# Experts sorted by token count on chip, whole float32 weights, and two column halves for small experts

## The chip, the cores and the metric

The kernel runs on one core of a Trainium2 chip. The metric is the device time of one execution in microseconds (us), the median of several. The core has five engines with programs of their own: TensorE (PE: matmuls, with its weight loads shown as PEld), VectorE (DVE), ScalarE (ACT), GpSimd (POOL) and SyncE (SP, which here only issues transfers), and 16 DMA engines. Engines wait for one another by semaphores.

## The reference

One decoder layer over 512 tokens of width 1024: a mixer, then a mixture of experts, each with a residual, and a last RMSNorm. The change touches the second part only:

```python
def hierarchical_moe(h, w_router_group, b_router_group, w_router_expert, b_router_expert,
                     w_expert_gate, w_expert_up, w_expert_down):
    ...
    gp, gi = lax.top_k(group_p, 1)
    ...
    ev, ei = lax.top_k(ep, TOP_K)
    ev = ev / jnp.sum(ev, axis=-1, keepdims=True)
    weights = gp * ev
    expert_id = gi * EXPERTS_PER_GROUP + ei
    combine = jnp.sum(jax.nn.one_hot(expert_id, N_EXPERTS, dtype=jnp.float32) * weights[..., None], axis=1)
    ...
    for e in range(N_EXPERTS):
        hid = jax.nn.silu(t @ w_expert_gate[e]) * (t @ w_expert_up[e])
        out = out + combine[:, e:e + 1] * (hid @ w_expert_down[e])
```

There are 32 experts in 4 groups; each token goes to 2 experts of one group, so there are 1024 pairs, 32 per expert on average. Gate and up are 1024 x 256, down is 256 x 1024, all float32: three matrices of 1.05 MB, 3.146 MB per expert, 100.7 MB in all.

## The kernel before

Everything is written engine by engine by hand; nothing is scheduled by a tool. After the mixer (some 470 us, untouched) the layer goes on as follows.

**Router.** TensorE transposes the normed tokens (`h2_tile`, L769) and makes the logits (L782). DVE picks group and experts by some 25 short operations (L2015 to L2047), TensorE counts how many earlier tokens chose the same expert (L812, L814: a token's rank in its expert), and DVE turns ranks into one-hot rows over 96 places (L2067). A product of those with the token numbers (L820) gives for each expert the up to 96 rows that it must read: `row_idx`. A token whose rank is 96 or more raises a flag (L2072 to L2095), and then a dense fallback computes all experts for all tokens at the end.

**Experts.** Experts are taken in the order 0 to 31, in a loop over groups of `UN` = 4, one buffer each (`wgu`, `wd`). All 32 have the same shape, 96 token rows, whatever their count. POOL gathers the rows from memory (L1190, `gather`; row numbers out of range are skipped) and writes the results back by a scatter (L1196, `scatter`). TensorE does per expert `e`: `ex_gu(e)` (gate and up side by side as 512 columns, 8 blocks of 128 in depth), `ex_tr(e+1)` (8 transposes of the gathered rows, L839), `ex_dn(e-1)` (down: 2 halves of 512 columns x 2 blocks), `ex_ht(e)` (2 transposes of the hidden rows, L861). Results leave PSUM through ACT (silu L1584, `ex_y` L1606) and DVE (L2108).

**Split product.** A float32 product is made from three in the type float32r: each operand is cut into a high and a low part.

```python
                pe.matmul(o, wh, xh, start=first, stop=False)
                pe.matmul(o, wh, xl, start=False, stop=False)
                return pe.matmul(o, wl, xh, start=False, stop=last)
```

These are L402 to L404 (`split_product`), used all over the kernel. The parts of the expert weights are made on chip: high by ACT (`gu_hi_half` L1562, `dn_hi_part` L1589), low by DVE (`gu_lo_half` L2007, `dn_lo_part` L2112), two halves for gate and up and one piece for down; the rows' parts likewise (L1577, L2102, L1598, L2116). DVE and ACT make expert 0's parts before they go on with the router.

**Weight transfers.** SP issues them: expert 0 after the first half of the output projection, 1 and 2 after the second, 3 after the first gather, and expert e+4's gate and up (L1002, L1003) when `ex_gu(e)` is done, its down (L1006) when `ex_dn(e)` is. SP runs in order, so a wait for a down buffer also holds the next gate.

Two program places matter besides: the transformed tokens `h2T` are stored away for the fallback (L1026) before their space is used, and the end (L2184 on) reads both results of each token back, weighs and adds them, and norms.

## Time and profile before

| | us |
|---|---|
| three runs | 834.97, 835.1, 838.05 |
| median | 835.1 |
| span of the profiled execution, first to last instruction | 836.0 |
| TensorE busy | 762.9 (91%) |
| DVE busy | 579.6 (69%) |
| ACT busy | 487.2 (58%) |
| POOL busy | 267.4 (32%) |
| transfers | 163.47 MB, mean 196 GB/s |

The profiled execution's own time is known as its span; it lies 0.9 us above the median and within the runs. Matmuls overlap in the array: each is drawn with its full length, so starts are closer together than lengths say. A busy share says nothing of which wait ends last. The granted clock of TensorE has two levels, 1.00 (2.4 GHz) and 0.50 (1.2 GHz). A plain float32 matmul appears as two records, a float32r matmul as one.

### The profile page before, as it was taken

Reading aid. Unit: us, or ns where it says so; the run is one execution under the profiler, and the core shown is the slowest. Engines: PE = TensorE matmul, PEld = TensorE weight load, DVE = VectorE, ACT = ScalarE, POOL = GpSimd, SP = SyncE. Lnnn points to the kernel's source line nnn. Section 1 sums busy time; section 2 is a strip of 40 time slices with the busy share of each in tenths; the row PEclk is TensorE's granted clock in tenths of the full one; section 3 lists DMA queues with packets and bytes.
Section 4 is the critical chain, followed back from the end, with each engine's and each line's share of the span. In section 5 each row is a group of like instructions: output and inputs, shape, how many; then the busy total and the mean of one; then the engine's idle time right before and its main releaser. Section 6 shows DMA issues by size and latency. Waiting matters only on the chain.

```text
span 836.0 us, 11559 instructions
## 1 busy us (share of the span) xinstructions
PE 762.9 (91%) x4238; PEld 604.6 (72%) x4238; DVE 579.6 (69%) x762; ACT 487.2 (58%) x680; POOL 267.4 (32%) x173
## 2 busy tenths in 40 slices
PE   4999999989999999998999549999999999999950
PEld 3788888878877988886788436777777777677730
DVE  4259879896764235645933556888888888888937
ACT  6322663842545445545313426888888888788833
POOL 2145433421512323425500031443444334442110
PEclk9999999999999999999999859999999999999995
DMA  8924320310300202094205677999999999989316
GB/s 240 321 88 153 113 72 31 110 42 13 127 13 2 102 2 102 1 350 164 47 1 201 267 269 249 360 365 372 358 375 367 375 345 349 354 346 353 111 57 257
DMA packets 50841, 163.47 MB, mean 196 GB/s; under 512 B 11321, under 2 KB 15433, under 8 KB 42351
## 3 DMA queue, kind: packets, MB, share of 16 engines
q1 hardware_dynamic: 43566, 154.47, 50.0%
q0 software_dynamic: 7232, 8.43, 3.1%
q8 instruction: 28, 0.46, 0.2%
q14 instruction: 15, 0.11, 0.0%
HBM read 154.48 MB, written 25.17 MB: 215 GB/s over the span
## 4 chain that ended last, share of the span: by engine, by line
PE 81%; DVE 6%; ACT 5%; DMA 5%; issue 2%; POOL 1%; SPq 0%; POOLq 0%; DVEq 0%; ACTq 0%
PE bank L402 22%; PE bank L404 21%; PE bank L403 21%; PE bank L839 3%; DMA wgu<-in_w_expert_up_dram 3%; PE bank L530 2%; DVE arena L2184 1%; PE bank L561 1%; PE bank L551 1%; PE bank L733 1%; PE bank L718 1%; PE bank L475 1%; DVE gu_lo L2007 1%; PE bank L584 1%; PE bank L599 1%
## 5 line engine op out<-in xcount | busy, mean ns | idle before, releaser
L2007 DVE TENSOR_TENSOR gu_lo<-wgu,gu_hi 128x2048 fp32r<-128x2048 f32 x64 | 146.4, 2288 | 25.7 <-ACT gu_hi L1562 25.4
L1103 POOL TENSOR_TENSOR w_lo<-arena,w_hi 128x1024 fp32r<-128x1024 f32 x36 | 86.1, 2396 | 211.9 <-ACT w_hi L1234 211.9
L1562 ACT ACTIVATE gu_hi<-wgu 128x2048 fp32r<-128x2048 f32 x64 | 122.1, 1910 | 27.2 <-DMA wgu<-in_w_expert_up_dram 17.2
L402 PE MATMUL bank<-h_hi,w_hi 128*128 128x512 f32 x320 | 128.2, 401 | 0.4 <-DVE arena L1796 0.4
L404 PE MATMUL bank<-h_hi,w_lo 128*128 128x512 f32 x320 | 125.0, 391 | 0.0
L403 PE MATMUL bank<-h_lo,w_hi 128*128 128x512 f32 x320 | 124.6, 389 | 0.0
L1190 POOL DMA_INDIRECT arena<-h_rows,row_idx x32 | 78.9, 2465 | 94.5 <-DVE row_idx L2078 76.8
L402 PE MATMUL bank<-gu_hi,heT_hi 128*96 128x512 f32 x256 | 103.9, 406 | 3.0 <-DVE heT_lo L2102 2.3
L404 PE MATMUL bank<-gu_hi,heT_lo 128*96 128x512 f32 x256 | 102.1, 399 | 0.0
L403 PE MATMUL bank<-gu_lo,heT_hi 128*96 128x512 f32 x256 | 101.5, 396 | 0.0
L1196 POOL DMA_INDIRECT y_rows<-arena,row_idx x32 | 42.4, 1325 | 177.7 <-ACT arena L1606 177.7
L2112 DVE TENSOR_TENSOR dn_lo<-wd,dn_hi 128x2048 fp32r<-128x2048 f32 x31 | 71.0, 2292 | 13.2 <-ACT dn_hi L1589 12.4
L1708 DVE SCALAR_TENSOR_TENSOR bank<-arena,bank 128x512 f32<-128x512 f32 x116 | 78.7, 749 | 0.1
L404 PEld LDWEIGHTS bank<-h_hi,w_lo 128*128 128x128 f32 x320 | 60.1, 188 | 13.0
L402 PEld LDWEIGHTS bank<-h_hi,w_hi 128*128 128x128 f32 x320 | 60.1, 188 | 12.9 <-DVE arena L1796 0.6
L403 PEld LDWEIGHTS bank<-h_lo,w_hi 128*128 128x128 f32 x320 | 60.2, 188 | 11.6
L1589 ACT ACTIVATE dn_hi<-wd 128x2048 fp32r<-128x2048 f32 x31 | 59.3, 1914 | 0.0
L402 PEld LDWEIGHTS bank<-gu_hi,heT_hi 128*96 128x96 f32 x256 | 41.8, 163 | 20.8 <-DVE heT_lo L2102 2.6
L1234 ACT ACTIVATE w_hi<-arena 128x1024 fp32r<-128x1024 f32 x40 | 41.4, 1052 | 23.8 <-PE bank L404 21.8
L404 PEld LDWEIGHTS bank<-gu_hi,heT_lo 128*96 128x96 f32 x256 | 41.7, 163 | 18.3
L403 PEld LDWEIGHTS bank<-gu_lo,heT_hi 128*96 128x96 f32 x256 | 42.0, 164 | 16.2
L402 PE MATMUL bank<-dn_hi,hidT_hi 128*96 128x512 f32 x124 | 50.5, 408 | 0.0
(315 smaller groups left out, 1428.8 us busy)
## 6 DMA issues: line engine op xcount, KB each, us to landing
wgu<-in_w_expert_gate_dram SPq DMA_DIRECT2D x32, 1024.0 KB, 9.3
wgu<-in_w_expert_up_dram SPq DMA_DIRECT2D x32, 1024.0 KB, 19.9
wd<-in_w_expert_down_dram SPq DMA_DIRECT2D x32, 1024.0 KB, 14.9
arena<-in_w_in_dram SPq DMA_DIRECT2D x8, 2048.0 KB, 8.5
arena<-in_x_dram SPq DMA_DIRECT2D x8, 512.0 KB, 7.8
arena<-in_w_in_dram SPq DMA_DIRECT2D x4, 1024.0 KB, 10.5
y_rows<-arena SPq DMA_DIRECT2D x8, 512.0 KB, 10.6
arena<-in_w_out_dram SPq DMA_DIRECT2D x2, 2048.0 KB, 10.3
```

The source lines that it names most:

```text
L402: pe.matmul(o, wh, xh, start=first, stop=False)
L403: pe.matmul(o, wh, xl, start=False, stop=False)
L404: return pe.matmul(o, wl, xh, start=False, stop=last)
L1103: gp.tensor_tensor(as_raw(w_lo[pslot(s)], s), raw(s), as_raw(w_hi[pslot(s)], s).bitcast(F32), ALU.subtract)\
L1190: gp.indirect_dma_start(out=hs[e % NHS][0:CAP, :], out_offset=None, in_=h2_rows, in_offset=bass.IndirectOffsetOnAxis(ap=row_idx[0:CAP, 0, ...
L1196: gp.indirect_dma_start(out=y_rows, in_=ysb[e % 2][0:CAP, :], in_offset=None, out_offset=bass.IndirectOffsetOnAxis(ap=row_idx[0:CAP, 1, e: ...
L1234: act.activation(as_raw(w_hi[pslot(s)], s), raw(s), ACT.Copy).then_inc(S["w_hi"], 1)
L1562: act.activation(gu_hi[j % 2][:, :, ks, :], wgu[j][:, :, ks, :], ACT.Copy)\
L1589: act.activation(dn_hi, wd[j], ACT.Copy).then_inc(S["w_dhi"], 1)
L1708: ins = STT(out=into, in0=upad[:, i, t:t + T], scalar=par[:, o + t:o + t + 1], in1=prev, op0=ALU.mult, op1=ALU.add)
L2007: TT(gu_lo[j][:, :, ks, :], wgu[j][:, :, ks, :], gu_hi[j % 2][:, :, ks, :].bitcast(F32), ALU.subtract)\
L2112: TT(dn_lo[j], wd[j], high.bitcast(F32), ALU.subtract).then_inc(S["w_dlo"], 1)
```

## The change

Four things change in the expert stage.

1. **Order.** Positions `s` = 0 to 31 take the place of expert numbers. Positions 0 to 3 (`NFIX`) are experts 0 to 3. For the others DVE and TensorE count tokens, rank the counts (`count`, `keys`, `rank`), and make a permutation by which the rows of all experts are sorted (`rows_e`, `sorted`). Positions 8, 14, 20 and 26 take the four largest, the others follow by falling count. SP reads the expert number of a position from `order_i` and issues the load with it. Results of position `s` are found by `row_idx` and, for narrow positions, `row_half`.
2. **Whole weights.** No weight or row is cut into parts: `ex_gu` and `ex_dn` use plain float32 matmuls, and ACT and DVE do no splitting here. ACT copies the transposed rows (`heT_copy`, `hidT_copy`); DVE only multiplies.
3. **Widths.** The eight positions in `WIDE` have 96 rows as before. The other 24 have 64 (`NARROW`): up goes to partitions 0 to 63 of the bank and gate to 64 to 127, on the two column halves of the array, 256 columns each; the two 512-column halves of down likewise. A token of rank 64 or more in a narrow position raises the flag.
4. **Buffers.** Six weight buffers (`NSLOT`) in place of four, three for gathered rows (`NHS`) in place of four. The down matrix is laid out as one piece of 8 KB per partition instead of two of 4 KB. The last norm's gain is loaded at the end.

The core of the diff:

```diff
-    UN = 4
+    NFIX = 4
+    WIDE = (0, 1, 2, 3, 8, 14, 20, 26)
+    NARROW = 64
+    NSLOT = 6
...
-        e_slot = [R_EXP + i * ESLOT for i in (2, 0, 1)] + [R_RING]
-        gu_hi = [parts(f"gu_hi{i}", R_SIG + i * KT * T, 2, KT, DE) for i in range(2)]
-        gu_lo = [parts(f"gu_lo{j}", o, 2, KT, DE) for j, o in enumerate(e_slot)]
-        wgu = [parts(f"wgu{j}", o, 2, KT, DE, dt=F32) for j, o in enumerate(e_slot)]
-        wd = [parts(f"wd{j}", o + 2 * KT * DE, JE, D, dt=F32) for j, o in enumerate(e_slot)]
-        dn_hi = parts("dn_hi", R_UP, JE, D)
-        dn_hi_end = parts("dn_hi_end", R_SIG, JE, D)
-        dn_lo = [parts(f"dn_lo{j}", o + 2 * KT * DE, JE, D) for j, o in enumerate(e_slot)]
...
+        EGU = 2 * KT * DE
+        gu_at = [R_EXP + 2 * ESLOT, R_EXP, R_EXP + ESLOT, R_RING, R_SIG, R_UP]
+        dn_at = [R_EXP + 2 * ESLOT + EGU, R_EXP + EGU, R_EXP + ESLOT + EGU, R_RING + EGU, R_SIG + EGU, R_SIG + EGU + JE * D]
...
+        wgu = [at(o, 2, KT, DE) for o in gu_at]
...
+        wd = [at(o, JE, D) for o in dn_at]
...
-        NHS = 4
-        hs = [at(o, D) for o in (R_UP + JE * D, R_UP + JE * D + D, R_S2, R_MASK)]
+        heT = [at(o2 + i * KT * CAP, KT, CAP) for i in range(2)]
+        heT_n = [at(o2 + i * KT * CAP, KT, NARROW) for i in range(2)]
+        NHS = 3
+        hs = [at(o, D) for o in (R_S2, R_S2 + D, R_MASK)]
...
+        def outs(s):
+
+            return s + 1 + sum(i <= s for i in WIDE)
+
+        def rows_of(s):
+            return CAP if s in WIDE else NARROW
...
+            b = begin("count", ("keys", 1), 5)
+            for c in range(NT):
+                pe.matmul(b[:, 0:NE], ones, Mx[:, c, :], start=(c == 0), stop=(c == NT - 1))
+            for c in range(NT):
+                ins = pe.matmul(b[0:NE, NE:NE + 1], Mx[:, c, :], ones[:, 0:1], start=(c == 0), stop=(c == NT - 1))
+            end(ins, "count", "route_mm")
+
+            b = begin("rows", ("idx_ready", 1), 4)
...
+                ins = pe.matmul(b[0:CAP, 0:2 * NFIX], row_of[:, i // NT, i % NT, :],
+                                codes[:, i // NT, i % NT, :, 0:NFIX], start=(i == 0), stop=(i == 2 * NT - 1))
...
+            b = begin("rows_e", ("perm_ready", 4), 6)
+            for q in range(2):
+                for i in range(2 * NT):
+                    ins = pe.matmul(b[0:NE, q * CAP:(q + 1) * CAP], codes[:, i // NT, i % NT, q, :],
+                                    row_of[:, i // NT, i % NT, :], start=(i == 0), stop=(i == 2 * NT - 1))
+            end(ins, "rows_e", "route_mm")
+            b = begin("sorted", ("sorted", 4), 7)
+            wait(pe, "perm_ready", 4)
+            for q in range(2):
+                pe.matmul(b[0:CAP, q * NE:(q + 1) * NE], rows_e[0:NE, q, :], perm[0:NE, :], start=True, stop=True)
+            pe.matmul(b[:, 2 * NE:3 * NE], both_e[0:NE, :, :].rearrange("p a b -> p (a b)"), perm[0:NE, :], start=True,
+                      stop=True)
+            pe.matmul(b[0:1, 3 * NE:4 * NE], e_col[0:NE, :], perm[0:NE, :], start=True, stop=True)
+            ins = pe.matmul(b[:, 4 * NE:5 * NE], ones[0:NE, :], on_diag[0:NE, :], start=True, stop=True)
+            end(ins, "sorted", "route_mm")
+            for b in range(5):
                 wait(pe, *used[b])
...
+            def ex_tr(s):
+
+                n = rows_of(s)
+                wait(pe, f"ld_h{s % NHS}", 16 * (s // NHS + 1))
+                wait(pe, "heT", s)
                 for k in range(KT):
...
+                    if n == CAP:
+                        o = bank[k // 4][:, (k % 4) * CAP:(k % 4 + 1) * CAP]
+                    else:
+                        o = bank[s % 2][:, k * NARROW:(k + 1) * NARROW]
+                    ins = pe.transpose(o, hs[s % NHS][0:n, :].rearrange("p (q k) -> p k q", k=KT)[:, k, :], ident[0:n, 0:n])
+                ins.then_inc(S["ex_tr"], 1)
...
+            def ex_gu(s):
+
+                wait(pe, "heT", s + 1)
+                wait(pe, f"ld_g{s % NSLOT}", 32 * (s // NSLOT + 1))
+                wait(pe, "ex_hid", s - 1)
+                o = bank[2 + s % 2]
                 for k in range(KT):
-                    if k % KH == 0:
-                        wait(pe, "w_glo", 2 * e + 1 + k // KH)
-                    ins = split_product(bank[2 + j % 2][0:CAP, :], (heT_hi[:, k, :], heT_lo[:, k, :]),
-                                        (gu_hi[j % 2][:, :, k, :], gu_lo[j][:, :, k, :]), k == 0, k == KT - 1)
+                    if s in WIDE:
+                        ins = pe.matmul(o[0:CAP, :], heT[s % 2][:, k, :], wgu[s % NSLOT][:, :, k, :], start=(k == 0),
+                                        stop=(k == KT - 1))
+                    else:
+                        for i, w in enumerate((wu, wg)):
+                            ins = pe.matmul(o[i * NARROW:(i + 1) * NARROW, 0:DE], heT_n[s % 2][:, k, :],
+                                            w[s % NSLOT][:, k, :], start=(k == 0), stop=(k == KT - 1))
                 ins.then_inc(S["ex_gu"], 1)
...
+            def ex_dn(s):
+
+                wait(pe, "hidT", s + 1)
+                wait(pe, f"ld_d{s % NSLOT}", 16 * (s // NSLOT + 1))
+                if s in WIDE or s - 1 in WIDE:
+                    wait(pe, "ex_y", outs(s - 1))
+                elif s > 1:
+                    wait(pe, "ex_y", outs(s - 2))
+                if s in WIDE:
+                    for hf in range(NH2):
+                        for m in range(JE):
+                            ins = pe.matmul(bank[6 + hf][0:CAP, :], hidT[:, m, :],
+                                            wd[s % NSLOT][:, m, hf * HALF:(hf + 1) * HALF], start=(m == 0),
+                                            stop=(m == JE - 1))
+                        ins.then_inc(S["ex_d"], 1)
+                else:
                     for m in range(JE):
-                        dh, dl = (w[:, m, hf * HALF:(hf + 1) * HALF] for w in (high, dn_lo[j]))
-                        ins = split_product(bank[6 + hf][0:CAP, :], (hidT_hi[:, m, :], hidT_lo[:, m, :]), (dh, dl),
-                                            m == 0, m == JE - 1)
-                    ins.then_inc(S["ex_d0" if hf == 0 else "ex_d1"], 1)
...
-            NTRIP = NE // UN
-            ex_tr(0, 0, 0)
-            trip(0, first=True)
-            with pe.Fori(1, NTRIP - 1) as g:
-                trip(g)
-            trip(NTRIP - 1, last=True)
+                        for hf in range(NH2):
+                            ins = pe.matmul(bank[6 + s % 2][hf * NARROW:(hf + 1) * NARROW, :], hidT_n[:, m, :],
+                                            wd[s % NSLOT][:, m, hf * HALF:(hf + 1) * HALF], start=(m == 0),
+                                            stop=(m == JE - 1))
+                    ins.then_inc(S["ex_d"], 1)
+
+            ex_tr(0)
+            for s in range(NE):
+                ex_gu(s)
+                if s < NE - 1:
+                    ex_tr(s + 1)
+                if s == 0:
+                    b = begin("flag", ("flag_ready", 1), 5)
+                    wait(pe, "route_dif", 3)
+                    ins = pe.matmul(b[0:1, 0:1], ones[:, 0:1], ovf[:, 0:1], start=True, stop=True)
+                    end(ins, "flag", "route_mm")
+                    wait(pe, *used[6])
+                    wait(pe, *used[7])
+                else:
+                    ex_dn(s - 1)
+                ex_ht(s)
+            ex_dn(NE - 1)
 
 
             wait(pe, "flag_ready", 1)
-            wait(pe, "ex_y", 2 * NE)
+            wait(pe, "ex_y", outs(NE - 1))
...
+            wde = a["w_expert_down"][0].rearrange("e (p m) n -> e p m n", m=JE)
...
+            expert_gu(3, 3)
+            expert_dn(3, 3)
+            wait(sp, "st_h2", 16 * NT)
+            wait(sp, "st_h2T", 16)
+            wait(sp, "sorted", 1)
+            for s in range(NFIX, NE):
+                e = sp.value_load(order_i[0:1, s:s + 1], min_val=0, max_val=NE - 1)
+                wait(sp, "ex_gu", s - NSLOT + 1)
+                expert_gu(s, e)
+                if s >= NSLOT:
+                    wait(sp, "ex_d", outs(s - NSLOT))
+                expert_dn(s, e)
+            wait(sp, "ex_gu", NE - 3)
+            sp.dma_start(gain3, a["final_norm_gain"].partition_broadcast(P)).then_inc(S["ld_part2"], 16)
...
+            def scatter(s):
+                gp.wait_ge(S["ex_y"], outs(s))
+                if s == NFIX:
+                    wait(gp, "sorted", 3)
+                if s in WIDE:
+                    gp.indirect_dma_start(out=y_rows, in_=ysb[s % 2][0:CAP, :], in_offset=None,
+                                          out_offset=bass.IndirectOffsetOnAxis(ap=row_idx[0:CAP, 1, s:s + 1], axis=0),
+                                          bounds_check=2 * T - 1, oob_is_err=False).then_inc(S[f"st_y{s % 2}"], 16)
+                else:
+                    gp.indirect_dma_start(out=y_half, in_=ysb[s % 2][:, 0:HALF], in_offset=None,
+                                          out_offset=bass.IndirectOffsetOnAxis(ap=row_half[:, s:s + 1], axis=0),
+                                          bounds_check=2 * NH2 * T - 1, oob_is_err=False).then_inc(S[f"st_y{s % 2}"], 16)
+
+            for s in range(NHS):
+                gather(s)
```

TensorE, from the end of one expert's gate and up to the next expert's, in the loop before (expert numbers e; L402 to L404 gate and up repeat eight times, of which three rows stand here):

```order
L404 MATMUL bank<-gu_hi,heT_lo 96x512
L839 MATMUL bank<-arena 128x96 x8
L402 MATMUL bank<-dn_hi,hidT_hi 96x512
L403 MATMUL bank<-dn_lo,hidT_hi 96x512
L404 MATMUL bank<-dn_hi,hidT_lo 96x512
...
L861 MATMUL bank<-arena 128x96 x2
L402 MATMUL bank<-gu_hi,heT_hi 96x512
L403 MATMUL bank<-gu_lo,heT_hi 96x512
L404 MATMUL bank<-gu_hi,heT_lo 96x512
```

and in the changed kernel around position 4, the first narrow one (L889 wide gate and up, L893 narrow, L918 wide down, L925 narrow down, L878 and L903 the transposes):

```order
L889 MATMUL bank<-arena 96x512 x8
L878 MATMUL bank<-arena 128x64 x8
L918 MATMUL bank<-arena 96x512 x4
L903 MATMUL bank<-arena 128x96 x2
L893 MATMUL bank<-arena 64x256 x16
L878 MATMUL bank<-arena 128x64 x8
L918 MATMUL bank<-arena 96x512 x4
L903 MATMUL bank<-arena 128x64 x2
L893 MATMUL bank<-arena 64x256 x16
L878 MATMUL bank<-arena 128x64 x8
L925 MATMUL bank<-arena 64x512 x4
```

The order of the four steps is kept; 24 and 12 matmuls become 8 and 4, or 16 and 4 of half the rows.

TensorE between the logits and the first expert of the changed kernel; before, only the first two lines' kinds, one product of 8 (L820) and the flag stood here:

```order
L831 MATMUL bank<-arena 128x128
L833 MATMUL bank<-arena 128x96
L833 MATMUL bank<-arena 128x64
L833 MATMUL bank<-arena 128x32
L838 MATMUL bank<-arena 128x32 x4
L840 MATMUL bank<-arena 32x1 x4
L846 MATMUL bank<-arena 96x8 x8
L852 MATMUL bank<-arena 32x96 x16
L858 MATMUL bank<-arena 96x32 x2
L859 MATMUL bank<-arena 128x32
L861 MATMUL bank<-arena 1x32
```

The counts (L838, L840), the rows by expert (L852) and the permutation (L858 to L861) are new, and stand ahead of expert 0's transposes; the flag's product moved behind expert 0's gate and up.

## Rows read from the trace of the kernel before

**Rows 1.** The page: busy times, the chain that ended last, and costly groups of instructions

```profile
PE 762.9 (91%) x4238; PEld 604.6 (72%) x4238; DVE 579.6 (69%) x762; ACT 487.2 (58%) x680; POOL 267.4 (32%) x173
...
PE bank L402 22%; PE bank L404 21%; PE bank L403 21%; PE bank L839 3%; DMA wgu<-in_w_expert_up_dram 3%; PE bank L530 2%; DVE arena L2184 1%; PE bank L561 1%; PE bank L551 1%; PE bank L733 1%; PE bank L718 1%; PE bank L475 1%; DVE gu_lo L2007 1%; PE bank L584 1%; PE bank L599 1%
...
L2007 DVE TENSOR_TENSOR gu_lo<-wgu,gu_hi 128x2048 fp32r<-128x2048 f32 x64 | 146.4, 2288 | 25.7 <-ACT gu_hi L1562 25.4
...
L402 PEld LDWEIGHTS bank<-gu_hi,heT_hi 128*96 128x96 f32 x256 | 41.8, 163 | 20.8 <-DVE heT_lo L2102 2.6
```

**Rows 2.** Busy time of each engine by stretch, then clock, DMA share, GB/s

```profile
core 0: us, PE busy (x) PEld busy (x) DVE busy (x) ACT busy (x) POOL busy (x), PEclk, DMA share, GB/s
470.00:480.00 10.00, 1.92 (x18) 1.78 (x16) 8.55 (x20) 4.17 (x4) 0.00 (x0) 0.67 1.00 408
...
490.00:500.00 10.00, 3.30 (x15) 2.40 (x15) 6.53 (x20) 4.17 (x4) 6.83 (x5) 0.50 0.42 130
...
600.00:700.00 100.00, 99.94 (x492) 73.00 (x491) 88.63 (x76) 86.67 (x98) 41.60 (x22) 1.00 0.95 363
```

**Rows 3.** The chain in order of time, experts: start us, us, what

```profile
524.88 0.86 PE bank L839 x8
...
656.29 0.86 PE bank L839 x8
```

**Rows 4.** Timeline of TensorE inside one expert: start us, us, engine, line

```profile
600.90 0.39 PE L403 MATMUL bank<-dn_lo,hidT_hi 128*96 128x512 f32 x1
601.13 0.39 PE L404 MATMUL bank<-dn_hi,hidT_lo 128*96 128x512 f32 x1
```

**Rows 5.** The chain from 224 to 240 us: plain float32 products back to back

```profile
227.46 3.72 PE bank L530 x16
231.18 3.43 PE bank L637 x8
```

**Rows 6.** Timeline of TensorE in the triangular solve: small tiles, then the full array

```profile
258.36 1.20 PE L584 MATMUL bank<-arena 32*32 32x32 f32 x64
...
259.82 0.40 PE L403 MATMUL bank<-h_lo,w_hi 128*128 128x512 f32 x1
...
266.91 2.08 PE L584 MATMUL bank<-arena 64*64 64x64 f32 x32
...
287.43 1.45 PE L584 MATMUL bank<-arena 32*32 32x32 f32 x64
```

**Rows 7.** Timeline around the router: logits, splitting, row product, first two experts

```profile
468.24 3.68 PE L782 MATMUL bank<-arena 128*128 128x64 f32 x32
...
470.91 4.49 DVE L2007 TENSOR_TENSOR gu_lo<-wgu,gu_hi 128x2048 fp32r<-128x2048 f32 x2 [3.79 <-ACT gu_hi L1562]
475.32 0.30 DVE L2016 TENSOR_TENSOR arena<-bank,arena 128x144 f32<-128x144 f32 x1
...
487.49 2.79 PE L820 MATMUL bank<-arena 128*96 128x64 f32 x16 [4.28 <-DVE arena L2067]
...
498.69 0.74 PE L402 MATMUL bank<-gu_hi,heT_hi 128*96 128x512 f32 x1 [1.17 <-DVE heT_lo L2102]
...
506.92 0.43 PE bank L839 x4
...
507.37 0.42 DVE L2108 TENSOR_TENSOR arena<-arena,bank 96x256 f32<-96x256 f32 x1 [8.74 <-ACT arena L1584]
...
512.50 0.48 PE bank L402
```

**Rows 8.** Timeline at the last expert's result

```profile
806.38 0.59 ACT L1606 ACTIVATE arena<-bank 96x512 f32<-96x512 f32 x1 [0.81 <-PE bank L404]
```

**Rows 9.** DMA queues in 600 to 650 us; up weights to landing, 528 to 540, 700 to 730

```profile
q1 hardware_dynamic: 2963, 16.82, 88.1%
q0 software_dynamic: 1228, 1.79, 9.9%
...
wgu<-in_w_expert_up_dram SPq DMA_DIRECT2D x2, 1024.0 KB, 12.0
...
wgu<-in_w_expert_up_dram SPq DMA_DIRECT2D x3, 1024.0 KB, 22.7
```

More of the change, by code:

```diff
@@ L823, in _ @@
             end(ins, "rows", "route_mm")
-            b = begin("flag", ("flag_ready", 1))
-            wait(pe, "route_dif", 3)
-            ins = pe.matmul(b[0:1, 0:1], ones[:, 0:1], ovf[:, 0:1], start=True, stop=True)
-            end(ins, "flag", "route_mm")
-            for b in range(8):
+            b = begin("rows_e", ("perm_ready", 4), 6)
[3 more added lines that the diff above has]
+                                    row_of[:, i // NT, i % NT, :], start=(i == 0), stop=(i == 2 * NT - 1))
@@ L1050, in _ @@
             wait(sp, "st_y1", 16 * NE // 2)
-            wait(sp, "ex_d1", NE)
+            wait(sp, "ex_d", outs(NE - 1))
             wait(sp, "ov_over", 1)
@@ L1207, in _ @@
+            for s in range(NHS):
+                gather(s)
+            for s in range(NE):
+                if s + NHS < NE:
+                    gather(s + NHS)
+                if s > 0:
+                    scatter(s - 1)
             scatter(NE - 1)
@@ L1630, in _, with heT_copy @@
-            act.wait_ge(S["idx_ready"], 1)
-            act.wait_ge(S["st_h2"], 16 * NT)
-            act.wait_ge(S["st_h2T"], 16)
-            gu_hi_half(1, 0, 1, 0)
-            heT_copy(0, 0, 0)
-            trip(0, first=True)
-            with act.Fori(1, NE // UN - 1) as g:
-                trip(g)
-            trip(NE // UN - 1, last=True)
+            def heT_copy(s):
+                wait(act, "ex_tr", s + 1)
+                wait(act, "ex_gu", s - 1)
+                if s in WIDE:
+                    for half in range(2):
+                        ins = act.activation(heT[s % 2][:, half * KH:(half + 1) * KH, :],
+                                             bank[half][:, 0:KH * CAP].rearrange("p (k n) -> p k n", k=KH), ACT.Copy)
+                else:
+                    ins = act.activation(heT_n[s % 2], bank[s % 2][:].rearrange("p (k n) -> p k n", k=KT), ACT.Copy)
+                ins.then_inc(S["heT"], 1)
@@ L2136, in _ @@
-            gu_lo_half(1, 0, 1, 0)
-            heT_rest(0, 0, 0)
-            trip(0, first=True)
-            with v.Fori(1, NE // UN - 1) as g:
-                trip(g)
-            trip(NE // UN - 1, last=True)
+            for s in range(NE):
+                wait(v, "ex_sil", s + 1)
+                wait(v, "ex_ht", s)
+                o = bank[2 + s % 2]
+                if s in WIDE:
+                    ins = TT(hid[0:CAP, :], sil[0:CAP, :], o[0:CAP, DE:2 * DE], ALU.mult)
+                else:
+                    ins = TT(hid[0:NARROW, :], sil[0:NARROW, :], o[0:NARROW, 0:DE], ALU.mult)
+                ins.then_inc(S["ex_hid"], 1)
```

347 lines of the change are left out of this document (149 added, 198 removed).

## The prediction

> **What bounds the kernel now.** I read the page first: TensorE is busy for 91% of the span, and the three split-product lines hold 64% of the chain that ended last [rows 1]. A mean over the span hides stages, so next the windows [rows 2]. From 600 to 700 us TensorE is busy 99.94 of 100 us at clock 1.00, and in the same 100 us the DMA share is 0.95 at 363 GB/s. From 470 to 500 both are different: the router runs, TensorE is mostly idle and its clock falls to 0.50 (the 1.2 GHz level); that is a latency stage. Third, the chain through the experts [rows 3]: the eight transposes that open each expert start at 524.88 and at 656.29 with 14 periods between, 9.386 us each. The timeline fills such a period [rows 4]: a matmul of 512 columns starts every 0.233 us though each is drawn 0.39 us long, so pace, not duration, is the price. 36 matmuls x 0.233 = 8.4, the transposes 0.86, and about 0.13 is left for the two transposes of the hidden rows. TensorE is the bound, and DMA is close behind it: the landing time of the up weights grows from 12.0 us at 528 to 540 to 22.7 us at 700 to 730 [rows 9], so transfers fall slowly behind.
>
> **The product whole.** It removes ACT's high parts and DVE's low parts of all weights (64 of 2.3 us for gate and up on DVE alone [rows 1]). Under a TensorE that never idles they cover nothing but themselves: worth 0, except at the start. On TensorE 3 split matmuls become one of plain float32. The conv mean does four of those (128x512), recorded as 8, in 3.43 us [rows 5]: 0.857 each against 3 x 0.233 = 0.70. Whole float32 alone is thus **slower**: a wide expert costs 8 x 0.857 = 6.86 and 4 x 0.857 = 3.43, 10.29 us in place of 8.4. A 256-column record costs 3.72/16 = 0.233, a 512-column one 3.43/8 = 0.43: the price goes by columns.
>
> **Column halves.** A narrow expert issues gate and up as 16 matmuls of 256 columns and down as 4 of 512, each on half of the array's columns. One after the other that is again 10.29 us; fully beside each other 5.14. The trace of before has no halves that share all rows. Nearest is the triangular solve [rows 6]: 64x64 products, one place of the array at a time, take (2.08-0.19)/31 = 0.061 us per record. 32x32 products, which alternate between two places, take (1.20-0.19)/63 = 0.016, another time (1.45-0.19)/63 = 0.020 (0.19 is one record's own length past its start). Half the columns would be 0.030 if serial, so two places give 1.5 to 1.9 times. Longer matmuls should lie near the upper end, where what is fixed per record weighs less: I take 1.8, 5.72 us per narrow expert, with 2.0 and 1.5 as ends of the range. These places share neither rows nor columns, so 1.0 is a rival. The Trainium skill ("TensorE: Matmul & The Clock Gate", Part 3, Measured speedup vs the span model) gives 2.38 times for three column tiles, 0.79 of ideal; for two that is 1.59 by my estimate, and the sum below would end at 810. No row here shows it.
>
> Going from the 32x32 places to the full array costs 259.82-0.233-259.38 = 0.2 us [rows 6]; a narrow expert has four such changes. Bounds 0 and 0.2, I take 0.1 each: 24 x 0.4 = 9.6 us.
>
> **The start.** DVE splits expert 0's weights before it turns to the logits [rows 7]: 470.91 to 475.32, while the logits are ready at 468.24+3.68 = 471.92. Gone, this gives 3.4 us, and the row product ends at 486.9 instead of 487.49+2.79 = 490.3. Then the sort is added: the transposed rows (32 records; the row product takes 2.79 for 16, less its last record's length 0.16 each: 5.2), two copies (0.6), the permutation (10 records and its hand-over: 1.9), the last two estimated from the same rows. The transposes of expert 0 stand behind them on TensorE, so they start near 494.6; the gather's flight is covered. 1.5 for them at the low clock and 1.2 for two ACT copies: gate/up of expert 0 starts at 497.3 against 498.69. It is 16 records x 0.43 = 6.9, plus 2.6 for the low clock (before: 8.2 for 24 x 0.233 = 5.6): 506.8. With transposes and expert 0's hidden rows (0.86 + 0.3), expert 1 starts at **508.0**. Before it was 512.5, since it waited for its split. The remaining router work on DVE (order, indices, codes, weights: 27 operations, none wider than the logits' 0.30 us) takes at most 9 us and ends by 504, before the first hidden rows need DVE.
>
> **The sum for TensorE from 508.0.** Wide gate/up 7 x 6.86 = 48.0; wide down 8 x 3.43 = 27.4; narrow 24 x 5.72 = 137.2; row transposes 30 x 0.86 = 25.8 (fewer columns, same weight loads); hidden transposes 31 x 0.2 = 6.2 (0.13 each before, a little more at a change of mode); changes 9.6; last hidden rows and copy, uncovered, 1.5. Together 255.7, so the last matmul ends at 763.7. Before it ended at 806.4 and the rest took 836.0-806.4 = 29.6 [rows 8], which the change leaves. Span 793.3. The span stands 0.9 above the median of the three runs (835.1), so **792 us**.
>
> Covered: silu and product are done 0.87 us after gate/up ends (506.92 to 507.79) [rows 7] and lie under the next transposes and down product (0.86 + 1.9). POOL is busy 41.6 us of 100 over 10.65 experts [rows 2], 3.9 each, which fits under 7. If that cover fails, each narrow expert grows by up to 1.
>
> **DMA under it.** In 600 to 650 us, 16.82 MB of weights is 5.35 experts, at 88.1% of 50 us: 8.2 us of all engines per expert, and 9.9% for indirect rows: 0.9 [rows 9]. From 470 to 480, with nothing indirect under way, 408 GB/s were moved [rows 2]: 3.146 MB/408 = 7.7. So 8.6 to 9.1 us per expert with rows. The sort reads its first number near 495, when expert 3's loads (issued near 492) still run, so the queue does not dry: 29 experts x 8.6 to 9.1 = 249 to 264, from 492. The wide experts at the front add gaps of about 5, since slots come free only every 11.5 us and SP waits in order (down's slot, then the next gate): last weights at 746 to 761. Six slots let DMA be five experts ahead at 550; it loses about 1 us per narrow run of the order and is not caught before the end. Thus 763.7 stands, but with little to spare.
>
> **Rivals.**
> - *Halves run one after the other.* The mechanism is shown only for places with different rows. Each narrow expert then costs 4.57 us more: 24 x 4.57 = 110, **902 us**, slower. It decides from a speed-up under 1.23 (24 x (10.29/1.23-5.72) = 43). For it: nothing here shows shared rows. Against: 1.9 times for the places shown. Chance 0.10.
> - *Weight loads are not hidden between halves.* A narrow expert has 40 records, each with a load; at 0.061 us each (the pace of the 64x64 records) 2.4 us on top of 5.14, so 24 x 1.82 = 44 more: **836 us**, no change. For it: twice as many loads per us as now. Against: in the full array loads of 163 ns vanish under a 0.233 us pace [rows 1]. Chance 0.07. The skill's rule in the same Part 3 (The mechanism) is that a load overlaps a running matmul only when its row group differs, or goes to the background buffer; the first half of it speaks against this change, and the full array's rows here show loads hidden with no row group differing.
> - *DMA becomes the bound at its present pace.* 29 x 9.4 = 273 from 492, gaps 5, last down and copy 4: 774 + 29.6 - 0.9 = **803 us**. For it: the share of 0.95 and the growing landing times. Against: 408 GB/s was reached. Chance 0.12.
> - *An expert above 64 tokens lands in a narrow position* and the dense fallback runs, over all experts and tokens: well above a millisecond. From the reference's routing, the four largest of experts 4 to 31 have 74, 66, 62 and 59 tokens, the next 57, so it can't with this input. Chance 0.01.
>
> **The numbers.** My case has 0.70. Its own ends: speed-up 2.0 and free changes of mode, 13.7 + 9.6 less, 769; speed-up 1.5 (164.6 in place of 137.2) and 0.2 per change, 37 more, 829. With DMA's 803 inside, the range 768 to 828 leaves 0.18 out. About 0.5% (4 us) is what a measurement tells here. Faster: 0.70 + 0.12 = 0.82. The 836 case is split: same 0.04, slower 0.03; with serial and fallback slower is 0.14.
>
> **What would show it.** Right: narrow gate/up takes 3.8 us for 32 records, wide 6.9; transposes every 11.5 and 7.0 us; no splitting operations; gate/up of expert 1 near 508; last matmul near 764; DMA share near 0.95 or above. Wrong: narrow gate/up of 6.9 us (serial) or 5 (loads exposed); TensorE waiting for DMA on the expert weights with its clock falling to 0.50 in the second half (DMA bound); a long wait for the order before expert 4's loads.

## The result and the profile after

| | before | after |
|---|---|---|
| median us | 836.0 (4 runs, 834.97 to 838.05) | 796.1 (4 runs, 794.36 to 798.44) |
| span of the profiled execution | 836.0 | 792.6 |
| TensorE, DVE, ACT busy | 762.9, 579.6, 487.2 | 726.7, 330.5, 292.4 |
| transfers | 163.47 MB | 163.61 MB |

Ratio 0.9535, interval [0.9515, 0.9555]: faster by 4.7%, 40 us. Forecast: 792 in 768 to 828.

The page of the changed kernel; the groups are line, engine, operation, out<-in xcount | busy, mean ns of one | idle before:

```profile
PE 726.7 (92%) x4296; PEld 528.3 (67%) x4296; DVE 330.5 (42%) x591; ACT 292.4 (37%) x536; POOL 211.7 (27%) x193
...
PE 85%; DVE 5%; ACT 4%; issue 3%; POOL 1%; DMA 1%; POOLq 0%; ACTq 0%; DVEq 0%; SPq 0%
...
L893 PE MATMUL bank<-arena 128*64 128x256 f32 x768 | 91.2, 391 | 5.2 <-issue 5.2
```

Against [rows 1], DVE lost 249 us of work and TensorE 36. All splitting of expert weights is gone, and TensorE's 36 us are most of the 43.4 us between the two spans. That fits the prediction's view that work under TensorE's cover was worth nothing by itself; no run leaves out the splitting alone. New is the 5.2 us of idle in front of L893, the narrow gate and up.

The chain through the experts, in order of time (start us, us, what), answers to [rows 3]:

```profile
505.01 6.88 PE bank L889 x16
511.88 0.86 PE bank L878 x8
512.74 3.44 PE bank L918 x8
516.18 0.20 PE bank L903 x2
516.38 6.87 PE bank L889 x16
...
594.54 3.60 PE bank L893 x32
598.14 1.02 PE bank L878 x8
599.16 1.87 PE bank L925 x8
601.03 0.38 PE bank L903 x2
601.41 3.60 PE bank L893 x32
```

A wide expert takes 516.38-505.01 = 11.37 us, a narrow one 601.41-594.54 = 6.87, against 9.39 for every expert before. Narrow gate and up, on two column halves, take 3.60 us where the wide ones take 6.88 (1.91 times), and down takes 1.87 where the wide one takes 3.44 (1.84). These ratios set 64 token rows against 96; the experiments below compare equal shapes. Eight wide and 24 narrow experts average 8.0.

Windows of the changed kernel (us, busy time of each engine, then granted clock, DMA share, GB/s), against [rows 2]:

```profile
480.00:490.00 10.00, 7.96 (x48) 7.62 (x48) 3.21 (x16) 0.00 (x0) 3.01 (x3) 0.50 0.87 318
490.00:500.00 10.00, 8.81 (x30) 4.48 (x31) 5.51 (x29) 0.87 (x2) 1.04 (x1) 0.83 0.87 325
500.00:550.00 50.00, 48.60 (x190) 23.14 (x190) 2.23 (x6) 12.78 (x27) 7.55 (x8) 1.00 1.01 379
...
600.00:650.00 50.00, 50.00 (x312) 26.79 (x310) 2.48 (x6) 12.15 (x28) 12.76 (x13) 1.00 1.02 387
650.00:700.00 50.00, 48.64 (x304) 26.65 (x301) 2.61 (x7) 11.77 (x27) 12.78 (x14) 1.00 1.02 391
700.00:740.00 40.00, 36.94 (x193) 19.39 (x193) 1.94 (x5) 8.49 (x19) 7.83 (x8) 0.91 1.00 397
```

Two things are to be read. DMA works at a share of 1.0 from 500 to about 735. And TensorE, which after one wait of 1.40 us at 503 to 504.6 (the first silu, see the last part) was not idle again until 650, then misses 1.4 of 50 and 3.1 of 40 us, with its clock at 0.91. Its timeline shows where (start us, us, engine, line, operation, and in brackets the idle time before):

```profile
687.44 3.67 PE L893 MATMUL bank<-arena 128*64 128x256 f32 x32
...
695.75 3.67 PE L893 MATMUL bank<-arena 128*64 128x256 f32 x32 [1.36 <-issue]
...
705.76 6.65 PE L893 MATMUL bank<-arena 128*64 128x256 f32 x32 [3.06 <-issue]
...
756.16 3.67 PE L893 MATMUL bank<-arena 128*64 128x256 f32 x32 [0.77 <-issue]
...
762.47 1.94 PE L925 MATMUL bank<-arena 128*64 128x512 f32 x8 [0.54 <-ACT arena L1676]
```

Three products of gate and up begin late, and the one after the 3.06 us wait takes 6.65 us in place of 3.67, at the lower clock. That is 1.36 + 3.06 + 2.98 + 0.77 = 8.2 us. The releaser is only "issue", so the trace doesn't name late weights. It does leave little else: such a product waits in the program for the copy of its transposed rows, for its gate and up weights, and for an older expert's hidden rows. Before the wait from 702.70 to 705.76 the copy was done at 701.08 and the hidden rows at 700.28. The experiments have to confirm it.

### The profile page after: what moved, and what is told of

Read it like the earlier page. It is cut to its first block, busy times and chain, and to the rows that moved or that the text cites. A ratio compares the mean times of both kernels' runs of the same rounds, so it can differ in the third digit from the quotient of the medians.

```text
span 792.6 us, 11110 instructions
## 1 busy us (share of the span) xinstructions
PE 726.7 (92%) x4296; PEld 528.3 (67%) x4296; DVE 330.5 (42%) x591; ACT 292.4 (37%) x536; POOL 211.7 (27%) x193
## 2 busy tenths in 40 slices
DMA packets 45218, 163.61 MB, mean 206 GB/s; under 512 B 9771, under 2 KB 13883, under 8 KB 32622
## 4 chain that ended last, share of the span: by engine, by line
PE 85%; DVE 5%; ACT 4%; issue 3%; POOL 1%; DMA 1%; POOLq 0%; ACTq 0%; DVEq 0%; SPq 0%
PE bank L421 13%; PE bank L423 12%; PE bank L422 12%; PE bank L893 11%; PE bank L889 7%; PE bank L925 6%; PE bank L878 4%; PE bank L918 4%; PE bank L549 2%; PE bank L903 1%; DVE arena L2239 1%; PE bank L580 1%; PE bank L570 1%; PE bank L752 1%; PE bank L737 1%
## 5 line engine op out<-in xcount | busy, mean ns | idle before, releaser
L893 PE MATMUL bank<-arena 128*64 128x256 f32 x768 | 91.2, 391 | 5.2 <-issue 5.2
L893 PEld LDWEIGHTS bank<-arena 128*64 128x64 f32 x768 | 56.2, 140 | 31.3 <-issue 7.7
L1283 POOL DMA_INDIRECT y_rows<-arena,row_half x24 | 24.3, 1011 | 133.1 <-ACT arena L1688 133.1
L889 PE MATMUL bank<-arena 128*96 128x512 f32 x128 | 58.3, 609 | 1.0 <-ACT arena L1656 1.0
L1268 POOL DMA_INDIRECT arena<-h_rows,row_idx x32 | 30.9, 966 | 91.8 <-DVE row_idx L2130 69.5
L925 PE MATMUL bank<-arena 128*64 128x512 f32 x192 | 46.5, 604 | 0.5 <-ACT arena L1676 0.5
L889 PEld LDWEIGHTS bank<-arena 128*96 128x96 f32 x128 | 20.8, 168 | 32.3 <-issue 30.9
L878 PEld LDWEIGHTS bank<-arena 64*128 64x128 f32 (+1 forms) x256 | 30.9, 201 | 14.3 <-issue 14.3
L878 PE MATMUL bank<-arena 64*128 64x64 f32 (+1 forms) x256 | 35.0, 277 | 0.0
L1217 POOL TENSOR_TENSOR b_lo<-arena,b_hi 128x512 fp32r<-128x512 f32 x16 | 25.6, 1601 | 31.0 <-ACT b_hi L1561 31.0
## 6 DMA issues: line engine op xcount, KB each, us to landing
y_rows<-arena SPq DMA_DIRECT2D x8, 512.0 KB, 10.3
```

The source lines that it names most:

```text
L878: ins = pe.transpose(o, hs[s % NHS][0:n, :].rearrange("p (q k) -> p k q", k=KT)[:, k, :], ident[0:n, 0:n])
L889: ins = pe.matmul(o[0:CAP, :], heT[s % 2][:, k, :], wgu[s % NSLOT][:, :, k, :], start=(k == 0), stop=(k == KT - 1))
L893: ins = pe.matmul(o[i * NARROW:(i + 1) * NARROW, 0:DE], heT_n[s % 2][:, k, :], w[s % NSLOT][:, k, :], start=(k == 0), stop=(k == KT - 1))
L925: ins = pe.matmul(bank[6 + s % 2][hf * NARROW:(hf + 1) * NARROW, :], hidT_n[:, m, :], wd[s % NSLOT][:, m, hf * HALF:(hf + 1) * HALF], star ...
L1268: gp.indirect_dma_start(out=hs[s % NHS][0:n, :], out_offset=None, in_=h2_rows, in_offset=bass.IndirectOffsetOnAxis(ap=row_idx[0:n, 0, s:s ...
```

## The experiments

All ratios are to the kernel before on the same chip. The diffs are shortened: semaphore counts and indices that follow from the lines shown are left out. The changed kernel itself came twice:

> The changed kernel again, unaltered, beside the three others of this series: 796 within 2 us, ratio 0.9535. It shows how far the waits of TensorE at the end (1.36 at 694, 3.06 at 703, 0.77 at 756, and a cold product behind the second) repeat from run to run.

Measured 796.05 us, ratio 0.9526 [0.9513, 0.9539]. Waits again lie near 697, 707, 750 and 758 (1.11, 3.19, 1.51, 0.80). Its profiled gate/up of expert 0 began 2.1 us later (495.5 in place of 493.4), and its last matmul ended 2.0 us later (766.4 in place of 764.4). Such shifts ahead of the experts are from run to run, and here the late waits did not absorb them. Counted from the sort's first transpose (L831, at 477.45 and 475.37), the last matmul ends after 289.0 us in both, and this count is used below.

### Where the gain is from: the two halves

```diff
-    WIDE = (0, 1, 2, 3, 8, 14, 20, 26)
+    WIDE = tuple(range(32))
```

> All 32 experts treated as wide (96 rows, no column halves); whole weights, order by count, the six buffers and the down layout of the change stay. Theory A (the gain is the two column halves): a wide period in the changed kernel's trace is 11.4 us (505.01 to 516.38), so from expert 1 at 505.0 to the last matmul 31 x 11.4 = 353, last matmul 858, span about 886, time about 885 to 890: worse than the kernel before (835), since its two-part experts took 10.3 on 64 columns or fewer of moving work. The share of DMA falls to 0.6 to 0.7 and no PE wait for weights is left. Theory B (the gain is larger transfers and deeper buffers, the halves only ride on it): 800 to 820.

Measured 892.8 us, ratio 1.0701 [1.0672, 1.0729], a little over the forecast of 885 to 890. Whole float32 weights without halves are 7% **slower** than the kernel before. Everything else in the change, taken together, doesn't make up for the plain product, which costs more than the split one: 11.4 us for each expert against 9.39 before (not 10.3, as the expectation has it).

```diff
-  ins = pe.matmul(o[i * NARROW:(i + 1) * NARROW, 0:DE], ...)
+  ins = pe.matmul((o, bank[5])[i][0:NARROW, 0:DE], ...)
```

(ACT's silu then reads gate from there.)

> Narrow experts keep 64 rows and 256-wide matmuls, gate and up alternating per piece, but both products use columns 0 to 63 of the array (gate's result goes to another bank). Nothing else changes. Theory A (two different column halves run side by side): the 32 matmuls of a narrow gate/up take 6.9 to 7.1 us in place of 3.60, plus 3.3 us on each of 24 narrow experts = 79 us, less the 6 to 9 us of waits for weights that vanish, so 865 to 870. Theory B (narrow tiles are cheaper by themselves, or the order of the records is what helps): group stays near 3.6 us and the time within 1% of 796.

Measured 869.7 us, ratio 1.0428 [1.0401, 1.0454], inside 865 to 870. Its timeline of TensorE:

```profile
561.63 0.45 PE L903 MATMUL bank<-arena 64*128 64x64 f32 x2
562.01 7.12 PE L893 MATMUL bank<-arena 128*64 128x256 f32 x32
569.06 1.09 PE L878 MATMUL bank<-arena 64*128 64x64 f32 x8
570.09 1.94 PE L925 MATMUL bank<-arena 128*64 128x512 f32 x8
```

The same 32 records, same shapes, same order, all in one half: 7.12 us in place of 3.67. In the chain, where overlaps are taken off, it is 7.05 in place of 3.60, 1.96 times. So place, and not tile size, is what pays for gate and up; no run puts the two halves of down on one place. This is also the price of the first rival, had it been true, for gate and up alone.

```diff
-  for k in range(KT):
-      for i, w in enumerate((wu, wg)):
+  for i, w in enumerate((wu, wg)):
+      for k in range(KT):
```

> Narrow gate/up products stay on their two column halves, but all eight pieces of up are issued first and then all eight of gate, in place of up and gate in turn. Theory A (the engine issues in order and two halves overlap only where neighbouring matmuls are on different halves): 32 matmuls take 6.8 to 7.1 us, as on one half: 865 to 870. Theory B (each half has a queue of its own that reaches far ahead): 3.6 us stays, 796.

Measured 853.4 us, ratio 1.0224 [1.0204, 1.0243], below A's forecast and far from B's. 32 records took 6.32 us:

```profile
562.09 6.32 PE L894 MATMUL bank<-arena 128*64 128x256 f32 x32
568.34 1.09 PE L878 MATMUL bank<-arena 64*128 64x64 f32 x8
```

Neither theory had the 0.80 us that is won. It could sit at the one change of half or at the end of the group, so the next kernel has three changes:

```diff
+  for h in range(2):
+      for i, w in enumerate((wu, wg)):
+          for k in range(4 * h, 4 * h + 4):
```

> Narrow gate/up: up pieces 0 to 3, then gate 0 to 3, then up 4 to 7, gate 4 to 7, each half of the array as in the change. With all eight of one in a row the group took 6.32 us, against 7.12 on one half and 3.67 in turn; so at the one seam 0.80 us was won, about four records' worth (a pair of records on two halves takes 3.67/16 = 0.23 where one alone takes 7.12/32 = 0.22). Theory A (the engine looks only a few records ahead across a change of half; each seam wins 0.8): three seams, 7.12 - 3 x 0.80 = 4.72, so 24 x (6.32 - 4.72) = 38 us less than 853, 815 to 818. Theory B (the 0.80 came once per group, at its end, where it meets the transposes, and not at the seam): 6.32 stays, 853.

```profile
563.91 0.45 PE L905 MATMUL bank<-arena 64*128 64x64 f32 x2
564.29 4.70 PE L895 MATMUL bank<-arena 128*64 128x256 f32 x32
568.92 1.13 PE L878 MATMUL bank<-arena 96*128 96x96 f32 x8
```

4.70 us against 4.72 forecast, and 814.8 us (ratio 0.9775 [0.9752, 0.9799]), at the edge of 815 to 818. Each change of half overlaps 0.80 us of work, about 3.6 records of 0.22 us, whether 8 or 16 records stand on either side. With two records in turn the overlap is nearly whole. **The overlap comes from the order of the program**: placing two products on two halves is not enough, they have to alternate within a few records. Why it reaches just so far is not shown.

### What the late waits are

```diff
-  wait(pe, f"ld_d{s % NSLOT}", 16 * (s // NSLOT + 1))
+  wait(pe, f"ld_d{s % NSLOT}", 16)
...
-  if s >= NSLOT:
-      wait(sp, "ex_d", outs(s - NSLOT))
-  expert_dn(s, e)
+  if s < NSLOT:
+      expert_dn(s, e)
```

> Down weights are loaded for the first six experts only; the later ones multiply with what stands in the buffer (their results are others), so from expert 6 on a third of the expert bytes is left out. TensorE's work is the same. Theory A (at the end the weights come late: PE waited 1.4 us at 694, 3.1 us at 703, then ran a cold product of 6.65 in place of 3.60, and 0.8 at 756): these go, last matmul at 755 to 758 in place of 764.4, span 784 to 787, time 3.5 to 9 us less than the changed kernel, 787 to 792; DMA share in 650 to 700 under 0.85. Theory B (those waits come from hidden y stores or from TensorE's own rhythm): 796 within 2 us and the waits stay.

Measured 787.65 us, ratio 0.9425 [0.9402, 0.9448], 8.4 us under the control. Not one of the waits is left. The tables of waits from 550 to 760 (us in all, times, longest) have one entry for TensorE's matmuls, in the changed kernel and in this one:

```profile
PE bank L893 <- issue: 5.2, 3, 3.1
```

```profile
PE bank L925 <- ACT arena L1675: 0.5, 1, 0.5
```

Its timeline, at the products that were late before:

```profile
703.31 3.67 PE L893 MATMUL bank<-arena 128*64 128x256 f32 x32
...
756.11 1.94 PE L925 MATMUL bank<-arena 128*64 128x512 f32 x8 [0.55 <-ACT arena L1675]
```

Fewer bytes, same arithmetic: the waits were for weights, and cost 8 us. The reason is a rate. A narrow expert wants 3.146 MB in 6.87 us = 458 GB/s, a wide one 3.146/11.37 = 277; delivered are 387 to 397 from 550 on, rows and results included. Before, one expert in 9.39 us wanted 335. The Trainium skill ("DMA: Bandwidth & Descriptors", Measured) gives 425 GB/s for a transfer of 16 MB with the neighbour core idle, and about 358 with both busy. The rows here lie between, and bear out that a lone core passes 358. By either figure narrow experts outrun the transfers.

```diff
-    NSLOT = 6
+    NSLOT = 4
```

> Four weight buffers instead of six; loads of an expert are then issued at most three experts ahead. Theory A (with whole experts at 6.87 us each and transfers at 8.2 us for 3.15 MB, the two extra buffers are what lets the wide, slow experts at the start pay for the narrow ones later): the queue idles during the wide ones, share falls below 0.95 in 500 to 550, and the lost megabytes (2 x 3.15 MB of lead, 16 us) come back as PE waits, time 805 to 813. Theory B (three experts ahead are enough, as the wide ones are spread out): 796 to 800.

Measured 808.6 us, ratio 0.9686 [0.9667, 0.9704], as A has it: the two extra buffers are worth 12 us. Its windows and first late product:

```profile
500.00:550.00 50.00, 48.60 (x168) 22.30 (x167) 2.23 (x6) 11.24 (x24) 6.65 (x7) 0.95 0.70 243
...
616.82 5.36 PE L893 MATMUL bank<-arena 128*64 128x256 f32 x32 [3.04 <-issue]
```

The share is 0.70 while the wide experts run, and TensorE waits from 616 on.

```diff
-  hid[0:n, :].rearrange("p (q m) -> p m q", m=JE)[:, m, :]
+  hid[0:n, m * P:(m + 1) * P]
...
-  wde = ...rearrange("e (p m) n -> e p m n", m=JE)
+  wde = ...rearrange("e (m p) n -> e p m n", m=JE)
```

> The down weights are laid out as before the change, two 4 KB pieces for each partition in place of one of 8 KB (and the hidden rows transposed to match); all else is the change. Theory A (transfers are the bound late, and pieces of 8 KB move at a better rate: 363 GB/s before at a share of 0.95, 385 to 390 after at 1.0): the late waits grow, from 5 us of PE waits to 8 to 15, time 799 to 806. Theory B (piece size makes nothing at this load): 796 within 2.

Measured 798.3 us, ratio 0.9585 [0.9553, 0.9618], just under A's range of 799 to 806. That is 2.2 us over the control by the medians and 5 us by the ratios; its interval overlaps that of the changed kernel's first series. In 600 to 650 it moved 375 GB/s in place of 387 at the same share, and five waits of 9.8 us in all stand where the changed kernel had three of 5.2 and the control four of 6.6. The waits grew as A has it; that the time grew is likely but not clear of the noise. The edit also changed TensorE's own work, which the expectation left out: the two hidden transposes of a narrow expert take 0.27 us in its chain in place of 0.38, so 24 of them are 2.6 us lighter. The price of the smaller pieces may be larger by that.

### Starting the transfers earlier

```diff
-  sp.dma_start(h2T_keep, h2T...).then_inc(S["st_h2T"], 16)
```

(and SP's wait for its end)

> Left out: the store of h2T (2 MB) that SP issues before the expert loads, and the wait for it; only the path for overflowing experts, which does not run here, would read it. Theory A (the transfers are the bound from about 500 on, at a share of 1.0 and 385 GB/s, and what is late at 694 to 756 is late by all that went before): 2.1 MB at 385 GB/s is 5.4 us earlier, the PE waits at 694, 703 and 756 (1.4, 3.1, 0.8, with the cold product 3.0 behind the second) nearly vanish, time 788 to 792. Theory B (the late loads are held by buffers coming free, not by the transfers): 796 within 2.

Measured 795.5 us, ratio 0.9532 [0.9516, 0.9548]: nothing, A's number falls. The windows say where the 2 MB went:

```profile
480.00:490.00 10.00, 7.94 (x54) 7.79 (x54) 4.62 (x21) 0.00 (x0) 1.87 (x2) 0.50 0.44 180
490.00:500.00 10.00, 8.31 (x36) 4.97 (x34) 5.98 (x30) 0.87 (x2) 2.17 (x3) 0.74 0.81 303
```

The store lay in time in which SP waits for the rows of expert 0 before it issues expert 3; without it the queue is idle instead. So that wait goes, alone:

```diff
-  wait(sp, "ld_h0", 16)
   expert_gu(3, 3)
```

> SP no longer waits for the rows of expert 0 (ld_h0) before it issues the loads of expert 3; the store of h2T stays in front. Theory A (the transfers are the bound from the start of the experts to the last load, so only idle time of the DMA engines ahead of it counts): the share of 0.87 in 480 to 500 goes to 1.0, 2.6 us of transfers earlier, time 793 to 795. Rival B (the wait was worth having: the gather of expert 0's rows, issued 485.7 to 488.4, now queues among 3 MB of weights and lands later than 491.3, and all of TensorE's experts begin later by that): start of the first gate/up at 496 to 499 in place of 493.4; as the late waits have 8 us to absorb it, 794 to 798.

and together with the store, which the overflow path then replaces:

```diff
-  sp.dma_start(h2T..., h2T_keep)
+  sp.dma_start(h2T[:, k, c * P:(c + 1) * P],
+      h2_rows[c * P:(c + 1) * P, :].rearrange("n (p k) -> p k n", k=KT)[:, k, :], ...)
```

> As the last, and h2T is neither stored nor waited for; the path for overflow rebuilds it from the rows of h2 that are in memory anyway (not run with these inputs). Without the early loads the left-out store gave nothing, as its 2 MB lay in time in which SP waited for ld_h0 (share 0.44 in 480 to 490). Theory A (transfer bound, idle time ahead counts): expert 3's 3.1 MB fill 482 to 490, and all later loads are 2.1 + 1.0 MB = 8 us ahead of the changed kernel's; the late waits vanish as with the lighter loads (787.7), so 787 to 790. Theory B (what is late at 694 to 756 is set by buffers coming free or by one slow DMA engine): 793 to 796.

Measured 796.45 (ratio 0.9532 [0.9517, 0.9548]) and 797.6 us (0.9544 [0.9531, 0.9557]). Neither gains. The first lies in rival B's 794 to 798; for the second A's 787 to 790 is clearly wrong, and the time lies just above B's 793 to 796. The timeline of TensorE and the windows, of the first:

```profile
495.71 1.52 PE L878 MATMUL bank<-arena 96*128 96x96 f32 x8 [2.45 <-DMA arena<-h_rows,row_idx]
498.19 8.80 PE L889 MATMUL bank<-arena 128*96 128x512 f32 x16 [0.96 <-ACT arena L1655]
```

```profile
490.00:500.00 10.00, 5.86 (x29) 3.92 (x28) 5.97 (x30) 0.87 (x2) 1.91 (x2) 0.67 1.03 361
500.00:550.00 50.00, 48.60 (x172) 22.64 (x171) 2.23 (x6) 11.43 (x24) 6.64 (x7) 0.98 0.94 343
```

and of the second:

```profile
480.00:490.00 10.00, 7.94 (x54) 7.80 (x54) 4.14 (x19) 0.00 (x0) 2.10 (x3) 0.50 1.01 423
490.00:500.00 10.00, 7.08 (x29) 4.16 (x28) 5.98 (x30) 0.87 (x2) 1.86 (x2) 0.67 0.68 245
500.00:550.00 50.00, 48.61 (x172) 22.63 (x171) 2.23 (x6) 11.53 (x25) 6.65 (x7) 0.99 0.91 326
```

The lead is won, and most of it is given back at once. Six buffers hold six experts and no more: the load for position 6 waits in every kernel until expert 0's gate and up is done, and is issued at 504.50 in the control, at 507.17 and 506.20 here. After it a buffer comes free only every 11.4 us while the wide experts run. So the share falls from 1.01 to 0.94 and 0.91, where the changed kernel's queue still has old loads to move. Second, rival B holds too: the gather of expert 0's rows shares the engines with 3 MB of weights, and TensorE waits 2.45 and 1.23 us for it. From the first gate/up to the last matmul both kernels are 2.6 and 2.7 us shorter than the control (498.2 to 766.5 and 496.6 to 764.9, against 495.5 to 766.4); but counted from the sort's first transpose, that gate/up begins 2.9 and 1.6 us later, which takes back all of it in the one and more than half in the other. From that transpose the last matmul ends after 289.3 and 287.9 us, against 289.0. I had read the share of 1.0 as "only bytes and rate count"; what counts is the rate and the six buffers that can hold a lead.

Last, the same with the silu's table brought ahead:

```diff
   act.activation(sm["tt"], sm["tt"], ACT.Exp)
+  act.activation(junk[:, 0:1], epsb, ACT.Silu)
```

> As the last, and a one-column Silu on ACT after the router's Exp brings its table in ahead, so that the 1.28 us of table load behind the first gate/up (502.3) is not waited for (PE idled 1.40 there). Theory A (with the transfers ahead TensorE is the bound, and each us off its path counts whole): 1.3 to 1.4 us below the run before, 786 to 789. Theory B (transfers still bound): no change against it.

Measured 794.9 us, ratio 0.9520 [0.9507, 0.9533]. That is not A's 786 to 789. Against the run before it is 2.7 us less by the medians and 0.24% by the ratios, whose intervals just overlap; TensorE's wait at the silu fell from 1.39 to 0.66 us. The late waits shrank to one, of 2.65 us at 714, with a product of 10.04 behind it that ran in part at the lower clock. Its median is 1.2 us under the control's, less than can be told. **No version that computes the whole layer was shown to be faster than the changed kernel.** Wide positions placed elsewhere, five buffers, and more than six were not tried.

## Why the prediction was right

The likeliest case came true, at 796 for 792, but one of the prediction's own signs of being wrong showed too: TensorE waited for expert weights and its clock fell to 0.50 (705 to 710). By its own steps:

- *Whole product slower.* 6.86 + 3.43 forecast from [rows 5], 6.88 + 3.44 measured; the kernel without halves lost 7%.
- *Column halves.* The one real guess, 1.8 times within 1.5 to 2.0, came out at 1.91 and 1.84 (1.96 for gate and up of equal shape), 5.47 us in place of 5.72 per narrow expert: 24 x 0.25 = 5.9 us too dear. That the longer matmuls lie near the upper end was the right choice. The rule of the Trainium skill ("TensorE: Matmul & The Clock Gate", Part 3, The mechanism) that a load overlaps a running matmul only when its row group differs, or goes to the background buffer, did not decide by its first half. Both halves share all rows, and 140 ns loads vanish (even in one half a record takes 0.22 us, half of a 512-column record's 0.43, so its load of 137 ns adds nothing). The estimate of 1.59, from the Trainium skill's figure for three column tiles ("TensorE: Matmul & The Clock Gate", Part 3, Measured speedup vs the span model), was too low. One sum of the first rival is wrong: at a speed-up of 1.23 the 24 narrow experts cost 24 x (10.29/1.23 - 5.72) = 63.5 us more, not 43; the change stops paying below 1.37. The measured speed-up is far from either.
- *Changes of mode.* Priced 9.6 us in all. Row transposes of narrow experts take 1.02 in place of 0.86, hidden ones 0.38 in place of 0.20, together 24 x 0.34 = 8.2 us. From the first gate/up of expert 1 (505.0) to the last matmul are 259.4 us; less the waits (8.2) and the three products (7 x 6.88 + 8 x 3.44 + 24 x 5.47 = 207.0) leaves 44.2 for transposes, changes and the end, where the prediction had 25.8 + 6.2 + 9.6 + 1.5 = 43.1. The lighter kernel, which has no waits, agrees: 507.1 to 758.05 is 250.9, and less 207.0 that is 43.9.
- *The start.* 508.0 forecast, 505.0 measured, but the logits already stood 2.7 us earlier in this profiled execution (465.53 against 468.24), ahead of anything changed. From the logits' end the parts fit: 15.0 us to the row product's end (15.0 forecast), transposes of expert 0 22.1 us after them (22.7 forecast). What the prediction missed is a table load on ACT, which before lay under expert 0's product at 498.06:

```profile
502.29 1.28 ACT L1667
503.57 0.01 issue
503.58 0.39 ACT arena L1667
```

  It now begins only when the product is done, and lies whole in the chain; bringing it ahead took half of the wait away.
- *DMA.* "Last weights 746 to 761, not caught before the end" is the **step that failed**, in its second half. Weights were still landing at the last gate/up (756.2), but TensorE did catch up, at 694. The price per expert was right: 29 experts from 491 to 745 or 756 are 8.8 to 9.1 us each, within the forecast's 8.6 to 9.1. Its lead was not: "about 1 us per narrow run" doesn't follow from those numbers, for six experts of 8.6 are 51.6 us against 5 x 7.0 + 11.5 = 46.5 on TensorE, 5 us lost in a run, and with 8.8 and 6.87 it is 7. Over four runs that eats three experts' lead. The third rival's mechanism thus came true to about half: 8 us over the 787.7 of the lighter kernel, where its 803 would have been 15.
- *The sum.* Last matmul 763.7 forecast, 764.4 measured: 3.0 us by the earlier start and 5.9 by the better halves, given back by 8.2 of waits and 1.4 in the rest. Two errors of opposite sign hid each other, and 2.7 of the 3.0 us are the luck of this execution, as said. The tail was 28.2 for 29.6. Of the 4 us between 792 and 796, 1.1 is in the spans: the four runs have 792.6, 793.9, 794.9 and 796.7, median 794.4, for 793.3 forecast. The rest is the step from span to time. In each of these runs the time is 1.7 to 1.8 us over its span, and 1.8 to 2.0 for the kernel before in the later series, where the prediction took 0.9 off; the span of 836.0 it went by fits the slowest run, 838.05, and not the median.

## To carry to other kernels

Two products of 64 columns or fewer over the same rows can run on two column halves at nearly twice the pace, if their matmuls alternate one by one (two records each here); then a plain float32 product beats a three-way split that costs two other engines besides (5.47 us for a narrow expert against 8.4). Once the arithmetic is faster than the memory, buy buffers (two more were worth 12 us here), spread the cheap tiles among the dear ones (no run varied that), and judge a transfer's worth by whether a buffer is free to take what moves up. A share of 1.0 on the queues isn't by itself a promise that an earlier start will end earlier.

## What the runs showed of the hardware

- Two column halves over the same 128 rows are 1.96 times as fast as one of them for the same 32 records (3.60 for 7.05 us in the chains), with a weight load for each record.
- The overlap reaches about 0.80 us, 3.6 records, across a change of half: 7.12, 6.32, 4.70 and 3.67 us for 0, 1, 3 and 15 changes in the same 32 records (the last 15 win 0.23 us each).
- The share of the DMA engines falls slowly at the end of the weights. The changed kernel's windows at its last weights:

```profile
735.00:740.00 5.00, 5.00 (x44) 3.17 (x41) 0.41 (x1) 1.06 (x3) 1.91 (x2) 1.00 0.88 352
740.00:745.00 5.00, 5.00 (x40) 2.66 (x36) 0.00 (x0) 0.77 (x2) 1.02 (x1) 1.00 0.79 318
745.00:750.00 5.00, 4.96 (x35) 3.03 (x35) 0.41 (x1) 1.75 (x4) 0.46 (x1) 1.00 0.54 223
750.00:755.00 5.00, 5.00 (x37) 2.87 (x33) 0.41 (x1) 0.98 (x2) 0.54 (x1) 1.00 0.37 150
```

  The last expert load was issued at 727.6 (after it only the last norm's gain, 0.5 MB at 738.5, and the rows), and the share falls over 20 us rather than at once, while the last gate/up still waits until 756.2. Engines that finish at different times would look so; the rows don't tell which engine is late, or why.
- A late weight can cost more than its wait. In these traces, after waits of 1.7 to 3.6 us the next product mostly took longer (6.65 us for 3.67, with a granted clock of 0.50 from 705 to 710, and 10.04 for 7.08), though not always (7.08 after 2.57 us, and after 1.77 with four buffers). After waits up to 1.6 us it never did.
